# One diffusion trunk layer stack: the modulation weights are loaded by rows instead of by columns, and the first layer's normalisation is written ahead of them

## What is computed

```python
mod_ctx = silu(c_ctx) @ w_mod[l] + b_mod[l]        # w_mod[l]: 1024 x 6144
mod_lat = silu(c)     @ w_mod[l] + b_mod[l]
sh1, sc1, g1, sh2, sc2, g2 = split(mod, 6)         # six vectors of 1024, two sets of them
h = rms_norm(x, norm1_g) * (1 + sc1) + sh1
parts = h @ w_in                                    # 1024 x 2656, split into four head groups
x = x + g1 * (concat(gating, convolution, retention, attention) @ w_out)
h2 = rms_norm(x, norm2_g) * (1 + sc2) + sh2
x = x + g2 * expert_choice_ffn(h2, router, w_gate, w_up, w_down)   # 16 experts
```

## Time and profile before

| | |
|---|---|
| median of 3 runs | 2107.55 us (2106.92 to 2109.28) |
| the profiled execution | 2113.24 us, of which its span in the trace is 2111.4 us |
| mean granted TensorE clock | 0.965 of full |
| PE busy | 1960.2 us, 93% of the span |
| layer 0 / layer 1 | the first expert starts at 517.3 us / 1547.3 us |

### The profile page before, as it was taken

How to read it: one execution, slowest core, us unless ns; L and a number is a source line. 1 busy time by engine, 2 the same in 40 slices (tenths; PEclk the granted TensorE clock), 3 DMA queues, 4 the chain that set the end, 5 groups by cost and what they waited for, 6 DMA issues and landing times.

```text
span 2111.4 us, 36634 instructions
## 1 busy us (share of the span) xinstructions
PE 1960.2 (93%) x15008; PEld 1099.3 (52%) x15008; DVE 525.9 (25%) x1193; ACT 471.9 (22%) x1031; POOL 150.5 (7%) x124
## 2 busy tenths in 40 slices
PE   5999999994999999999979999989879999999995
PEld 3756677882434444343456656778634443434342
DVE  1257122624111110111121841245421111111112
ACT  2232233222212111111131223332321111212112
POOL 0000001000010110101000000000001101011110
PEclk9999899996999999999989999999889999999998
DMA  9213123147899999999943122225449999999997
GB/s 307 84 58 120 41 81 103 68 175 285 327 390 393 385 394 389 390 393 390 388 143 119 64 80 80 68 76 207 171 179 384 392 391 390 392 390 394 386 397 250
DMA packets 210040, 533.78 MB, mean 253 GB/s; under 512 B 17072, under 2 KB 99376, under 8 KB 209712
## 3 DMA queue, kind: packets, MB, share of 16 engines
q1 hardware_dynamic: 191824, 493.52, 61.5%
q0 software_dynamic: 12288, 23.07, 5.1%
q10 hardware_dynamic: 5856, 16.16, 1.9%
HBM read 506.59 MB, written 26.12 MB: 252 GB/s over the span
## 4 chain that ended last, share of the span: by engine, by line
PE 68%; DMA 14%; SPq 8%; DVE 4%; issue 3%; ACT 2%; ACTq 0%; DVEq 0%; POOLq 0%
PE wide L1169 13%; DMA ring<-w_up 12%; PE wide L765 9%; PE wide L755 8%; PE wide L1177 7%; SPq L595 7%; PE wide L1047 7%; PE narrow L1200 6%; PE wide L1213 3%; PE turned L721 2%; PE wide L882 1%; PE narrow L701 1%; PE narrow L1070 1%; PE narrow L918 1%; PE wide L1188 1%
## 5 line engine op out<-in xcount | busy, mean ns | idle before, releaser
L1169 PE MATMUL wide<-ring,ht 128*64 128x512 f32 x2048 | 454.9, 599 | 9.5 <-DMA ring<-w_up 4.9
L1169 PEld LDWEIGHTS wide<-ring,ht 128*64 128x64 f32 x2048 | 143.7, 138 | 305.2 <-issue 278.5
L1177 PE MATMUL wide<-ring,ht 128*32 128x256 f32 x4096 | 234.3, 380 | 0.0
L1200 PE MATMUL narrow<-ring,ht 128*64 128x512 f32 x1024 | 233.8, 598 | 0.0
L2034 DVE TENSOR_TENSOR ht<-ht,wide 128x512 f32<-128x512 f32 x64 | 35.5, 554 | 680.4 <-ACT ht L1625 460.0
L765 PE MATMUL wide<-stream,ht 128*128 128x256 f32 (+1 forms) x960 | 192.4, 362 | 3.5 <-DVE ht L1704 3.5
L1177 PEld LDWEIGHTS wide<-ring,ht 128*32 128x32 f32 x4096 | 126.5, 110 | 108.2 <-issue 31.3
L765 PEld LDWEIGHTS wide<-stream,ht 128*128 128x128 f32 x960 | 169.4, 190 | 24.2 <-issue 4.0
L755 PE MATMUL wide<-ht,stream 128*128 128x128 f32 (+1 forms) x640 | 178.4, 441 | 0.0
L1625 ACT ACTIVATE ht<-wide 128x512 f32<-128x512 f32 x32 | 19.1, 597 | 623.4 <-PE wide L1169 623.4
L2200 POOL DMA_INDIRECT moe_sums<-ht x64 | 99.5, 1554 | 773.9 <-DVE ht L2051 695.5
(11 more groups left out here) (263 smaller groups left out, 1576.8 us busy)
## 6 DMA issues: line engine op xcount, KB each, us to landing
ring<-w_gate SPq DMA_DIRECT2D x256, 512.0 KB, 12.5
ring<-w_up SPq DMA_DIRECT2D x256, 512.0 KB, 14.1
ring<-w_down SPq DMA_DIRECT2D x128, 1024.0 KB, 19.7
stream<-w_mod SPq DMA_DIRECT2D x38, 1024.0 KB, 5.5
stream<-w_in SPq DMA_DIRECT2D x20, 1024.0 KB, 7.4
ring<-w_mod SPq DMA_DIRECT2D x10, 1024.0 KB, 12.0
stream<-w_out SPq DMA_DIRECT2D x6, 1024.0 KB, 5.9
moe_sums<-x ACTq DMA_DIRECT2D x10, 512.0 KB, 6.8
```

Source lines behind the costliest of these rows:

```text
L1169: ins = mm(psW[h * 64:(h + 1) * 64, 0, w * HALFW:(w + 1) * HALFW], xT[:, k, 0:CAPS], ring[:, k, w, h * HALFW:(h + 1) * HALFW], start=(k == ...
L1177: ins = mm(psW[q * STRIP:(q + 1) * STRIP, 1, w * QW:(w + 1) * QW], xT[:, k, CAPS:SLOTS], ring[:, k, w, q * QW:(q + 1) * QW], start=(k == 0 ...
L1200: ins = mm(psN[c * 64:(c + 1) * 64, 0, :], hmT[:, j, h_ * 64:(h_ + 1) * 64], ring[:, KD + k // 2, k % 2, c * HALFW:(c + 1) * HALFW], start ...
```

## The change

A unit is now a quarter of the rows, 256 of 1024, over all 1024 columns of one modulation vector: unit 4g + i holds rows 256i to 256i + 255 of vector g, in pieces of 4 KB. Strip q of the accumulator gets columns 256q to 256q + 255. The four units of a vector therefore belong to one sum. For vectors 0, 1, 2 and 5 (`HELD`) the sum is left in the accumulator over four units (job `group.g`); for 3 and 4, whose units lie between attention steps that use the other buffer, each unit is copied out by DVE and added to `mod_rows` (`mod.12` to `mod.19`). `mod_columns` runs once for a vector: one matmul that puts b_mod in, and two that spread the strips into columns; one instruction then writes `modT`.

Further: in layer 0 the norm up to the first half of the transposes (`norm_first`) stands ahead of `mod:0-8` on PE, and the same on DVE; layer 1 keeps its order. The parameters are split into the norm gains with b_mod (`load_gains`, 64 columns, first) and the rest, which in layer 0 is issued behind the first two pieces of w_in. PE waits for the rest at `latents` rather than at `in:mla`; DVE and ACT wait for it behind `norm_out`. Unit 20 moves from ahead of the output projection to behind `choose`, and `rows_g1` from behind `att_end` to ahead of it.

```diff
-STEPS += ["mod:18-21", "att_end", "rows_g1", "router_bias", "retention", "out", "choose", "mod:21-24", "tables", "rows_g2"]
+STEPS += ["mod:18-20", "rows_g1", "att_end", "modc:4", "router_bias", "retention", "out", "choose", "mod:20-24", "tables", "rows_g2"]
...
+PARTS = 4
+HELD = (0, 1, 2, 5)
+HELD_UNITS = [PARTS * g + i for g in HELD for i in range(PARTS - 1)]
+COLUMNS_AFTER = {MOD_FIRST - 1: (0, 1), 12: (2,), 16: (3,), MOD_UNITS - 1: (5,)}
...
+            def mod_part(l, u):
+
+                g, i = divmod(u, PARTS)
+                return mod_h[bass.ds(l, 1), :, 2 * i:2 * i + 2, g * D:(g + 1) * D].rearrange("l p k n -> (l p) k n")
+
+            def mod_used(l, u):
+
+                if mod_job(u):
+                    N.wait(sp, l, mod_job(u))
+                else:
+                    sp.wait_ge(s_mod, l * len(HELD_UNITS) + HELD_UNITS.index(u) + 1)
...
+            load_gains(0)
             for n in range(NSTREAM):
                 load_unit(0, n)
             for u in range(NSTREAM, MOD_FIRST):
                 load_head(0, u)
+            for n in (NSTREAM, NSTREAM + 1):
+                load_unit(0, n)
             load_params(0)
...
-                for k in range(KD):
-                    q = k % 4
-                    ins = mm(psN[q * STRIP:(q + 1) * STRIP, N.buf(job), 0:GW], sT[:, k, :], w[:, k, :], start=(k < 4), stop=(k >= 4))
-                N.finish(ins)
+                first, last = (i == 0, i == PARTS - 1) if g in HELD else (True, True)
+                if first:
+                    N.claim(pe, l, job)
+                for k in range(2):
+                    for q in range(PARTS):
+                        ins = mm(psN[q * STRIP:(q + 1) * STRIP, N.buf(job), 0:GW], sT[:, 2 * i + k, :], w[:, k, q * GW:(q + 1) * GW],
+                                 start=(first and k == 0), stop=(last and k == 1))
...
-                for c in range(NG):
-                    ins = mm(bank(N, job)[:, 2 * c:2 * c + 2], mod_rows[:, u % 2, c * P:(c + 1) * P], con("strips"), start=True, stop=True)
+                mm(o, ident, par("bmod")[:, KD * g:KD * (g + 1)].unsqueeze(2).broadcast_to([P, KD, 2]), start=True, stop=False)
+                for b in range(NG):
+                    ins = mm(o.rearrange("p (q b c) -> p b q c", q=PARTS, b=NG)[:, b], mod_rows[:, g % 2, b * P:(b + 1) * P],
+                             con("strips").rearrange("p (q c) -> p q c", q=PARTS), start=False, stop=(b == NG - 1))
...
                     if kind == "mod":
+                        if l == 0 and s == STEPS[0]:
+                            norm_first(l, "norm1")
                         modulation(l, *map(int, arg.split("-")))
...
+            def modulation(l, lo, hi):
+
+                for which, u in mod_steps(lo, hi):
+                    if which == "cols":
+                        if u < 2:
+                            job = f"modc.{u}"
+                            N.wait(dve, l, job)
+                            N.take(V.tensor_copy(modT[:, KD * u:KD * (u + 1), :].rearrange("p k c -> p (k c)"), bank(N, job)[:, 0:2 * KD]), job)
+                        continue
+                    g, i = divmod(u, PARTS)
+                    job = mod_job(u)
+                    if not job or 1 < g and g in HELD:
+                        continue
+                    N.wait(dve, l, job)
+                    dst, src = mod_rows[:, g % 2, :], bank(N, job)[:, 0:GW]
+                    if g in HELD or i == 0:
+                        ins = V.tensor_copy(dst, src)
+                    else:
+                        N.taken(dve, l, mod_job(u - 1))
+                        ins = V.tensor_tensor(dst, dst, src, ALU.add)
+                    N.take(ins, job)
```

More of the change, by code:

```diff
@@ L209 @@
 CONSTS = dict(ident=P, mean=P, expo=2 * P, mask=2 * P, qpos=2 * P, kpos=2, cos=TS * ROPE,
-              sin=TS * ROPE, eps=1, strips=2, rows=3)
+              sin=TS * ROPE, eps=1, strips=2 * PARTS, rows=3)
 def spans(sizes):
@@ L222 @@
 PAT, NPARAM = spans(PARAMS)
+NGAIN = PAT["bmod"][1]
 CAT, NCONST = spans(CONSTS)
@@ L607, in layer @@
             def layer(l, more):
-                for n in range(NSTREAM, NUNIT):
+                for n in range(NSTREAM + 2, NUNIT):
                     load_unit(l, n)
@@ L711, in mod_columns @@
                 N.finish(ins)
             def modulation(l, lo, hi):
-                for which, u in mod_order(lo, hi):
-                    (mod_unit if which == "mod" else mod_columns)(l, u)
+                for which, u in mod_steps(lo, hi):
+                    (mod_unit if which == "unit" else mod_columns)(l, u)
             def transposes(l, job, outs_ins):
@@ L722, in transposes, with norm_first @@
                 T.finish(ins)
-            def norm(l, which):
+            def norm_first(l, which):
                 pe.wait_ge(s_xn_act, (l + 1) * ACT_TILES)
@@ L734, in norm, with turn_sample, norm_rest @@
                     W.finish(ins)
-                for k in range(4, KD):
-                    job = f"{which}.{k}"
-                    o = bank(T, job)
-                    transposes(l, job, [(o[:, t * P:(t + 1) * P], xn[:, t, k * P:(k + 1) * P]) for t in range(TS)])
+                for k in range(4, 6):
+                    turn_sample(l, which, k)
+            def turn_sample(l, which, k):
+                job = f"{which}.{k}"
+                o = bank(T, job)
+                transposes(l, job, [(o[:, t * P:(t + 1) * P], xn[:, t, k * P:(k + 1) * P]) for t in range(TS)])
+            def norm_rest(l, which):
+                for k in range(6, KD):
+                    turn_sample(l, which, k)
                 for i in range(2):
@@ L1105, in router_bias @@
                 rt = par("router", KD, STRIP)
-                for u in (14, 15):
-                    N.taken(pe, l, f"modc.{u}")
+                N.taken(pe, l, "modc.3")
                 N.claim(pe, l, "bias.r")
@@ L1348, in norm_out, with mod_out @@
                 T.take(ins, job)
-            def mod_rows_out(l, u):
-                out(N, l, f"mod.{u}", mod_rows[:, u % 2, :], bank(N, f"mod.{u}")[:, 0:GW])
-            def mod_out(l, u):
-                job = f"modc.{u}"
-                N.wait(act, l, job)
-                for c in range(NG):
-                    j = NG * u + c
-                    ins = A(modT[:, j, :], bank(N, job)[:, 2 * c:2 * c + 2], ACT.Identity, bias=par("bmod")[:, j:j + 1])
-                N.take(ins, job)
-            def modulation(l, lo, hi):
-                for which, u in mod_order(lo, hi):
-                    (mod_rows_out if which == "mod" else mod_out)(l, u)
+            def mod_out(l, g):
+                out(N, l, f"modc.{g}", modT[:, KD * g:KD * (g + 1), :].rearrange("p k c -> p (k c)"), bank(N, f"modc.{g}")[:, 0:2 * KD])
+            def modulation(l, lo, hi):
+                for which, u in mod_steps(lo, hi):
+                    if which == "cols":
+                        mod_out(l, u)
+                    elif u // PARTS in HELD and mod_job(u):
+                        out(N, l, mod_job(u), mod_rows[:, (u // PARTS) % 2, :], bank(N, mod_job(u))[:, 0:GW])
             def rows_out(l, g, dst, func=ACT.Identity):
@@ L2254, in _constants @@
     put("rows", np.stack([SAMPLE * (p >= CAPS), p // CAPS, q + 4 * np.where(slot < CAPP, SAMPLE, NTOK + slot - CAPP)], 1))
-    put("strips", np.tile(np.eye(STRIP)[:, 0:2], (P // STRIP, 1)))
+    put("strips", np.stack([p == STRIP * q_ + c_ for q_ in range(PARTS) for c_ in range(2)], 1))
     put("eps", np.full((P, 1), EPS))
```

112 lines of the change are left out of this document (66 added, 46 removed).

## The result

The changed kernel takes 2092.23 us (median of 7 runs, 2085.85 to 2099.74), against 2107.55 before: a ratio of 0.9926, 95% interval 0.9912 to 0.9941, so 15.3 us faster. A second series of the same kernel gave 2090.32 and 0.9917 (0.9896 to 0.9938). The forecast was 2085.6, in a range from 2078 to 2097: the direction and the range hold, the gain is 15 to 17 us where 22.0 were summed.

What follows compares the result with a forecast made beforehand. PE, with 68% of the chain, was taken to bound the kernel, waits deciding in four places. Terms 6.1 + 5.5 + 4.6 + 3.8 + 2.0 = 22.0 us off 2107.55 gave 2085.6 us, range 2078 to 2097.

Steps and rivals of the forecast that it cites:

- The start: Layer 0 up to the projection: faster unit loads and earlier transposes, 8.7 us earlier, net 6.1; bounds 2 and 11.
- my old-path step: Layer 0, from ACT's next eviction to the projection: taken as unchanged from the old kernel, 5.84 us.
- The cold start: Layer 0's first projection: PE probably starts it at 1.2 GHz, with fewer transposes right ahead; costs 2.6 us.
- The columns: Dense part of each layer: fewer column sets on PE, net 2.7 us a layer, 5.5 in both; bounds 4 and 7.
- The end of attention: Unit 18 to the retention, 17.15 us before: 2.3 us less a layer, 4.6 in both; bounds 2.5 and 6.
- The gather: Expert 0's rows in layer 0: 7.0 instead of 10.8 us, parameters starting later; gain 3.8, bounds 5 and a loss of 3.
- Between the layers: Layer 0's last scatter: five shorter units leave the queue before it comes; gain 2.0 us, bounds 0 and 4.
- Rival (a): Start gives little: 4 KB slices no faster, projection cold, gather meets parameters; 12.1 us gained, 2095.5 us; chance 0.14.
- (b): Dense parts: DVE, emptying units of vectors 3 and 4, holds PE's next claim; about 2097 to 2106 us; chance 0.04.
- (c): Units on PE: the four strips stop overlapping, 2.5 us more for each of 32 units; slower, 2166 us; chance 0.02.

Runs made afterwards that it cites:

- g1_back: The changed kernel with the step rows_g1 moved back behind att_end and modc:4, before the router's bias; 2088.42 us, ratio 0.9912.
- next_late: The changed kernel with the next layer's loads issued only when expert 0's rows have been gathered; 2087.78 us, ratio 0.9892.
- params_early: The changed kernel with layer 0's parameters ahead of the first two pieces of w_in, as before; 2090.46 us.

## Why the forecast was right, and where its sum was off

**The start: right, net of the clock in part by luck.** The projection comes 7.6 us earlier, against 8.7; loads at 412 GB/s and the transposes ahead are in the rows. Most of the missing microsecond lies between ACT's next eviction (41.22) and the projection, 6.69 us where I carried over 5.84: PE starts the 16 late transposes only at 42.09, behind copies that my old-path step (49.66 to 55.50) had as already under way. The cold start, put at 2.6, costs 2.7 in the changed kernel's profile (29.05 less 26.34). It is no fixed price: with the same start the first pass takes 26.34 us in one kernel's execution and 29.39 in another's. Net, unit 8, which stands behind the first pass, comes 4.9 us earlier in the profiles of the changed kernel (76.96 and 76.88, before 81.84 and 81.76), and 4.6 to 7.8 in the others; 6.1 was forecast.

**The columns: right; what came on top is not shown to be theirs.** 2.7 a layer forecast; in layer 1 4.7 over the two pairs. Counted from the earlier trace rows, nine sets at 0.46 go and two come; a new set costs 0.69 as forecast, so the sets give 2.8, and at the same granted clock PE's busy time falls by 2.7 (249.70 to 247.05). The rest is idle time of PE (11.05 us against 9.56 and 9.28 in the same windows) and, in three of the four old layers, a lower clock. I cannot put the idle time down to one wait: ahead of the first attention value product PE waits 1.16 to 2.69 us in the four layers of the old profiles and 1.36 to 1.76 in the four new ones. Why the old kernel was granted less in this stretch stays open.

**The end of attention: right.** 2.1 and 2.6 us against 2.3. What can give them is the unit and the columns that left the stretch; `rows_g1` counts 3.77 us in the sum wherever it stands, and g1_back shows that its move gave nothing (14.56 us without it).

**The gather: the term that failed.** "The median of 32 gathers is 7.1" against 10.8 made 3.8 us; the gain is 0.2. Two steps were wrong. The 10.8 was one execution's: the stage took 13.07 us there and 9.39 in the other, where the gather landed in 7.1. DMA packets while the rows moved, first profile of the old kernel (506.5 to 513.7) and second (504 to 506.7):

```profile
DMA packets 476, 2.40 MB, mean 334 GB/s; under 512 B 38, under 2 KB 272, under 8 KB 352
```

```profile
DMA packets 484, 0.92 MB, mean 340 GB/s; under 512 B 30, under 2 KB 389, under 8 KB 469
```

124 packets of over 8 KB, the parameters, moved beside the rows in the first and 15 in the second: the collision that the forecast took away is there in one of two executions. And the price put in its place, 7.0, was too low: the parameters do move behind the gather now, as forecast, but beside the units, in 4 KB pieces, it took 8.3. Taken away, these too, it lands in 4.3 us, so the mechanism, contention, was the right one, but the change only replaced what the gather collides with.

**Between the layers: failed.** 2.0 against 0.2. The step that failed is that the units are what the scatter waits beside. The five units, issued from 1027.21 on, have all but left the queue when the scatter is issued at 1046.30, as forecast; but w_in is issued right behind them, at 1045.96, and the scatter runs beside that. With w_in and the unit behind it held back the scatter takes 3.71 us, as I had read it from layer 1.

**Not seen at all:** the retention of layer 0 at a lower clock, -2.2 us in both profiles of the changed kernel; in other kernels of the new order it lies elsewhere in the stage, and in layer 0 of next_late there is none.

That the total came within 5 to 7 us is in part luck: the dense stretches gave some 4.5 us more than forecast, and the gather, the stretch between the layers and the retention some 7.6 less.

Rival (a) had the start give little and came to 2095.5; the time lies between it and the sum, but for another reason: the start gave about what was forecast, and the gather and the stretch between the layers did not. Rivals (b) and (c) did not come: a unit in the dense part still takes 1.07 us (76.96).

## What to carry to other kernels

Before a stall's price goes into a sum, see it in two executions: the slow gather and the stretches at half clock differed by 2 to 4 us between profiles of one kernel, as much as the terms that they carried. For a transfer that is slow beside others, ask what the queue holds at that moment in the new order, not only what it held in the old one. In this kernel, bound by PE, some of PE's waits cost twice, once as idle time and once as half-rate matmuls behind them (expert 0: 15.87 and 16.50 us against 13.95); idle work that fits the wait gave the second part back, and twice as much of it cost more than it gave.

## What the runs showed of the hardware

The last scatter of layer 0 takes 8.27 us beside two pieces of w_in and 3.71 with them held back; the first gather takes 8.2 us beside units in 4 KB pieces and 4.3 without them, and beside the old kernel's loads 10.8 in one execution and 7.1 in another. Pieces of 1 KB moved at 349 GB/s and pieces of 4 KB at 412. PE's clock fell behind waits of 1.2 and 2.7 us between units (a unit of 1.07 us at 31.92, one of 1.93 at 34.72), and in 48 to 54 us, under dense matmuls, the mean grant was still 0.55 in one execution, while in params_early it was 1.00 through the whole first pass. With it the time of one stretch, from the first projection to unit 18 of layer 0, with the same instructions, lay between 282.2 and 287.2 us over the kernels of the new order.
